# Two decoder layers on one NeuronCore: chunks 0 and 1 become one group that reads its weights once

## The reference, cut to what matters

```python
h = rms(x, g_mix_norm[l])
x = x + mixer_block(h, ...)     # w_in: 1024 x 2816, four mixers of 4 heads, w_out: 1024 x 1024
h = rms(x, g_ffn_norm[l])
x = x + peer(h, w_peer_q[l], sub_keys[l], peer_u[l], peer_v[l])

def peer(h):                    # per chunk of 128 tokens
    q = (xc @ w_q).reshape(C, 8, 2, 128)                  # w_q: 1024 x 2048
    s = einsum('thpd,hpkd->thpk', q, sub_keys)            # 2 x 128 keys a head
    sv, si = top_k(s, 16)                                 # then top 16 of the 16 x 16 sums
    eidx, g = 16 experts of 16384 a head, softmax(top)
    a = einsum('thkd,td->thk', u_tab[eidx], xc)           # gathered rows of 1024
    return einsum('thk,thkd->td', g * gelu(a), v_tab[eidx])
```

## Time and profile before

| | |
|---|---|
| median of 3 runs | 3382.74 us |
| lowest and highest of them | 3364.05 and 3389.28 us |
| the profiled execution, span from first to last instruction | 3383.4 us |
| PE, DVE, POOL, ACT busy | 2560.1, 2327.2, 2291.7, 690.9 us |
| bytes moved | 1205.57 MB |

### The profile page before, as it was taken

The page is one execution under the profiler, slowest core; times in us unless marked ns, Lnnn a source line. Parts: engine busy times, 40 slices in busy tenths (PEclk is TensorE's granted clock), DMA queues, the critical chain, the costliest instruction groups (busy, mean ns, idle before and its releaser), DMA issues.

```text
span 3383.4 us, 27538 instructions
## 1 busy us (share of the span) xinstructions
PE 2560.1 (76%) x7696; PEld 1422.5 (42%) x7696; DVE 2327.2 (69%) x5442; ACT 690.9 (20%) x1655; POOL 2291.7 (68%) x2052
## 2 busy tenths in 40 slices
PE   6568777986777778877787787987787778666667
PEld 5545344743443435533353443643354334222222
DVE  2495678568689875666668886666668888655554
ACT  2112212123311111112211221123322122101011
POOL 0156766566667676676776777677777777777776
PEclk9789888988888888998899998998899899888888
DMA  5489999998899999998999999999999999999998
GB/s 235 174 320 406 358 377 371 343 378 310 308 376 367 347 344 407 401 379 332 352 394 369 379 373 348 390 397 344 348 358 397 363 382 368 368 367 359 366 366 336
DMA packets 316375, 1205.57 MB, mean 356 GB/s; under 512 B 37184, under 2 KB 37440, under 8 KB 301248
## 3 DMA queue, kind: packets, MB, share of 16 engines
q0 software_dynamic: 294912, 1073.87, 83.9%
q1 hardware_dynamic: 21312, 129.94, 9.7%
HBM read 1201.57 MB, written 2.10 MB: 356 GB/s over the span
## 4 chain that ended last, share of the span: by engine, by line
PE 30%; POOL 22%; issue 18%; DVE 17%; DMA 7%; ACT 3%; another core or an unknown queue 2%; SPq 0%; DVEq 0%; ACTq 0%; POOLq 0%
POOL ring L479 22%; PE psY L815 15%; PE psP L694 8%; DMA ring<-in_v,idx 6%; DVE ring L1067 5%; PE psP L689 4%; DVE x L1076 1%; DMA ring<-in_u,idx 1%; DVE sc L860 1%; PE psT L675 1%; ACT diag L656 1%; DVE hot L1031 1%; DVE hot L1032 1%; DVE pick L1033 1%
## 5 line engine op out<-in xcount | busy, mean ns | idle before, releaser
L815 PE MATMUL psY<-ring,diag 128*128 128x512 f32 x3120 | 1689.6, 685 | 678.0 <-DMA ring<-in_v,idx 270.3
L479 POOL DMA_INDIRECT ring<-in_u,idx x1024 | 1148.1, 1121 | 588.1 <-issue 304.3
L1067 DVE CUSTOM_DVE_ANT_0 ring<-ring,htok 128x1024 f32<-128x1024 f32 x1024 | 1232.4, 1223 | 450.5 <-DMA ring<-in_u,idx 396.5
L479 POOL DMA_INDIRECT ring<-in_v,idx x1024 | 1143.3, 1117 | 490.2 <-issue 284.2
L815 PEld LDWEIGHTS psY<-ring,diag 128*128 128x128 f32 x3120 | 636.9, 216 | 1545.9 <-issue 1087.1
L656 ACT ACTIVATE diag<-cst,wgt 128x128 f32<-128x128 f32 x780 | 275.5, 393 | 480.8 <-PE psY L815 184.9
L1076 DVE SCALAR_TENSOR_TENSOR x<-ring,wgt,x 128x1024 f32<-128x1024 f32 x244 | 313.6, 1285 | 39.5 <-DMA ring<-in_v,idx 27.6
L694 PE MATMUL psP<-wr,hT 128*128 128x256 f32 x1392 | 312.7, 383 | 5.1 <-DMA wr<-in_w_out 3.0
L689 PE MATMUL psP<-hT,wr 128*128 128x256 f32 (+1 forms) x1664 | 314.8, 350 | 0.7 <-ACT hT L517 0.7
L689 PEld LDWEIGHTS psP<-hT,wr 128*128 128x128 f32 x1664 | 282.2, 200 | 49.7 <-issue 23.1
L694 PEld LDWEIGHTS psP<-wr,hT 128*128 128x128 f32 x1392 | 267.6, 193 | 65.4 <-issue 22.9
(11 more groups left out here) (125 smaller groups left out, 1652.3 us busy)
## 6 DMA issues: line engine op xcount, KB each, us to landing
wr<-in_w_in SPq DMA_DIRECT2D x44, 1024.0 KB
wr<-in_w_q SPq DMA_DIRECT2D x40, 1024.0 KB
wr<-in_w_out SPq DMA_DIRECT2D x19, 1024.0 KB
ring<-in_u,idx POOLq DMA_INDIRECT x1024
ring<-in_v,idx POOLq DMA_INDIRECT x1024
ring<-in_w_in SPq DMA_DIRECT2D x11, 1024.0 KB, 13.2
x<-in_x SPq DMA_DIRECT2D x4, 512.0 KB, 20.1
sub<-in_subkeys SPq DMA_DIRECT2D x2, 1024.0 KB
```

The lines of the kernel that those rows point to most:

```text
L479: pool.indirect_dma_start(out=ring[:, q % NB], out_offset=None, in_=table, in_offset=bass.IndirectOffsetOnAxis(ap=idx[:, s % NS, n:n + 1], ...
L815: last = nc.tensor.matmul(psY[:, b * 512:(b + 1) * 512], diag[:, m % ND], r[:, b * 512:(b + 1) * 512], start=first, stop=final)
L1067: v.tensor_tensor_reduce(out=r, in0=r, in1=htok[:, s % NS], scale=1.0, scalar=0.0, op0=ALU.mult, op1=ALU.add, accum_out=adot[:, n:n + 1]). ...
```

## The change

The groups (0,) and (1,) become one group (0, 1). Its start slot is -148, where (0,) had -72 and (1,) had 22. Group (2, 3) starts at slot 104 and not 126, with a rate of 0.8 and not 0.7. The groups (4, 5) and (6, 7) are as they were. W_EARLY goes from 12 to 15, so that w_in and w_out of the first group pass through the ring. x of chunk 1 is loaded at the start beside x of chunk 0. (Blank lines at the head of the file go too.)

```diff
@@ -57,14 +38,14 @@
 DV, BV, SU, SV, CB = 4, 5, 6, 7, 8
 
 NB = 12
-W_EARLY = 12
+W_EARLY = 15
 NW = 2
 ND = 4
 NS = 3
 
 
 
-GROUPS = [((0,), -72, 1.0, 1.0), ((1,), 22, 1.0, 0.95), ((2, 3), 126, 0.7, 1.2), ((4, 5), 336, 1.15, 1.3),
+GROUPS = [((0, 1), -148, 1.0, 1.0), ((2, 3), 104, 0.8, 1.2), ((4, 5), 336, 1.15, 1.3),
           ((6, 7), 594, 0.97, 1.5)]
 GROUP_OF = {s: steps for steps, *_ in GROUPS for s in steps}
 
@@ -433,7 +414,8 @@
                 sp.dma_start(gain_f[:], g_ffn[l].partition_broadcast(P)).then_inc(s_late, 16)
                 sp.dma_start(sub[:], subkeys[l]).then_inc(s_late, 16)
 
-            sp.dma_start(x[:, 0], x_in[0:P]).then_inc(s_x[0], 16)
+            for c in range(2):
+                sp.dma_start(x[:, c], x_in[c * P:(c + 1) * P]).then_inc(s_x[c], 16)
             sp.dma_start(cst[:], cst_in).then_inc(s_cst, 16)
             parameters(0)
             for G, (s, i) in enumerate(PIECE_LIST):
@@ -444,7 +426,7 @@
                     late_parameters(l)
                 if G == NB // 2:
                     late_parameters(0)
-                    for c in range(1, NC):
+                    for c in range(2, NC):
                         sp.dma_start(x[:, c], x_in[c * P:(c + 1) * P]).then_inc(s_x[c], 16)
                 place, there, _, used = piece_at(G)
                 if used > 0:
```

## The result

The changed kernel takes 3471.03 us (median of 4 runs, 3463.08 to 3485.64), the kernel before 3383.59 (median of 4, 3364.05 to 3389.28). The ratio is 1.0271, with a 95% interval of 1.0233 to 1.0308. It is slower by some 87 to 92 us; the forecast was 3479, 95 us slower. The profiled execution of the changed kernel took 3463.08 us and has a span of 3461.3, so it is the fastest of its four, and the two spans stand only 77.9 us apart. I come back to that difference.

The account below looks back on a forecast made before the run. A chain of small dependent steps up to the first gather, then a gather stream limited mostly by DMA, was taken as the bound. 3383.4 + 127.4 (later first gather) + 1 - 36 + 3 = 3479 us, range 3440 to 3508.

Parts of the forecast that it names:

- (a) to (d): Before the first gather: later start +9.1, w_in +38.6, chunk 0's attention +4.9, chunk 1's mixers +50.5 us.
- (e) to (g): Before the first gather: w_out +12.4, second norm +8.2, first w_q piece +3.7 us.
- DMA was to stand at 0: Ahead of the stream: DMA at 0 between about 60 and 250 us but for single pieces.
- (d): Before the first gather: chunk 1's mixers, all new on the path, +50.5 us, bounds 40 and 60.
- Slots 0 to 72: Start of the stream: DVE decides, not DMA; 236 us from first gather to slot 72, 235 before, so +1.
- Slots 72 to 123: Stream with no front left in it: 148 us where it took 184, so -36.
- plain pace: Gather stream without front or weights: 1.44 us a gather, 2.88 a slot; 88 us above it before group (2, 3) begins.
- +3 for (2, 3): Group (2, 3) starting 22 slots earlier, its pieces crowding PE: +3 us, bounds 0 and +15.
- Rival 1: DMA sets the whole stream, so bytes count: 23.1 MB fewer give back 58 us, time 3453; chance 0.20.
- price of 1.9 us a piece: Stream between 240 and 340 us: a weight piece cost 1.9 us where DMA was the limit.
- Rival 2: The stream gives nothing back, as DVE choices and earlier (2, 3) pieces crowd it: 3511 us; chance 0.12.
- rival 3: Not slower: chunk 1's mixers run beside chunk 0's and the stream gives 77 us: 3383 us; chance 0.06.

Follow-up runs that it names:

- spread: Changed (merged) kernel with the choices of pairs of group (0, 1) spread over 1.5 times as many slots; ratio to the kernel before 1.0184.
- late23: Changed (merged) kernel with group (2, 3) put back to start slot 126 and rate 0.7; ratio to the kernel before 1.0288.
- thin: Kernel before with the 23 weight loads of chunk 1's group cut to an eighth of their columns, in 128-byte pieces; ratio 1.0014.
- thin1k: Kernel before with the 23 weight loads of chunk 1's group cut to one block of rows, 1 KB a partition; ratio 0.9974.
- delay: Kernel before with 130 DVE copies, about 61 us, put before the first choice of pairs, so the first gather is later; ratio 1.0170.
- mix36: Changed kernel with group (0, 1)'s mixers starting at unit 36, not 50, under the last w_in pieces, start slot -134; ratio to the kernel before 1.0253.
- before_again: Kernel before run once more, unchanged, for a trace from the same chip as other runs; ratio 1.0009.
- combo: Changed kernel with the edits of spread and mix36, and 2 of 16 v rows on DVE for heads 0 to 4, not 4; ratio to the kernel before 1.0156.

## Why the prediction was right

**The bound.** Two stages, with a chain of dependent steps up to the first gather and DMA mostly behind it. The chain of stage one was right in each term to about 2 us. Measured ends: w_in pieces begin at 29.4 (forecast 28.9); the last one ends at 112.8 (112); "stick out" of chunk 0 ends at 142.5 (140.4); that of chunk 1 ends 52.5 behind it (50.5); from the first w_out product to the last addition 30.4 (31.4); from there to w_q 16.1 (16.4); the first w_q piece 9.6 (10.2). The sum was 127.4, and 129.8 and 127.7 were measured in the two pairs. The small errors partly cancel: (a) to (d) came some 4 us above the forecast and (e) to (g) 2 us below. The first w_out piece began at 204.4 and not between 198 and 201. And one sign was wrong: DMA was to stand at 0 from about 60 us on, but had a share of 0.46 from 60 to 80 us and 0.33 from 80 to 100, and stopped only at about 112, as pieces come no sooner than PE frees their places.

**(d), the second chunk's mixers.** It was the largest term and was a sum of pieces, so it is worth a look. Head 1's scores came 9.5 us behind "stick out" (9.6 forecast). The heads followed at 3.81 us (155.83 - 152.02) and 3.89, where I had 3.2: each step works on rows twice as wide, and the two records of the scores took 1.22 us at the lower clock (granted 0.50 from 150 to 165 us, with PE busy for 9.51 of the 15). That makes 1.3 of the 2 us; the rest lies behind the last scores.

**Slots 0 to 72.** Forecast 236, measured 236.1. DVE decides, as was said, but that the number fits to a tenth is luck: the forecast was 10.6 us to the first dot product, 215 of work and 10 of waits, and the trace has 8.3, 209 and 18. Against the kernel before it is -5.6 and not +1, since before needed 241.7; its 235 in the prediction came from 143 records counted in two stretches, one of them twice; by 376 us 71 dot products had begun, and slot 72 began at 382.4. spread shows by experiment that DVE paces this stretch.

**Slots 72 to 123.** Forecast -36, measured -25.5 (178.2 to 152.7). The plain pace is reached only if (2, 3) stays away, as late23 shows (147.0). The +3 for (2, 3) was thus too low up to slot 123; in slots 123 to 144 one pair of traces took 5 us less than before and the other 3 more. Together with slots 0 to 72: forecast -32, measured -31.1 and -31.5. That agreement is luck in part: the errors of the two stretches, 6 to 7 us one way and 10 the other, cancel but for the 3 of (2, 3).

**Behind slot 123.** The prediction had the rest of the stream unchanged and +3 for (2, 3). The crowding of PE by the pieces of (2, 3) did cost 6 to 12 us up to slot 123, but slots 144 to 304 then took 12 to 16 us less, which no term of the prediction has.

**Rival 1 fell**, but not by the result alone: in the two profiled executions of the result the whole stream is 51.9 us shorter, near its 58, and in the pair from one chip 37.7. It fell by thin and thin1k. The bytes were priced at 58 us (61 with the pieces counted right, 96 in the stream before and 73 after, as 19 are read ahead of the first gather in both), and thin1k gives 8.5 and thin nothing for 21.1 MB. The Trainium skill's sentence in "DMA: Bandwidth & Descriptors", section "Issuing engines are not separate DMA queues", agrees with the traces as a statement on the engines: with the weights gone, their share fell from 0.96 and 0.98 in delay to 0.90 and 0.94 in thin1k. But a gain in time needs more, that nothing else waits in that stretch. My own price of 1.9 us a piece, from the rows between 240 and 340 us, was too high as well: 22 pieces would be 42 us. So most of the stream's saving needs the engine work of chunk 1's front to go ahead of the stream. Which engine or wait that work held up between slots 72 and 123 wasn't separated: PE and DVE were each busy for 76% there.

**Rival 2 fell** by the 31 us, and **rival 3** by the first gather: the order of the lists holds, and mix36, which loosens it in one place, has its first gather 7 us sooner.

**The whole.** The stream gave back about 31 us up to slot 123, and 35 up to slot 144 in late23, where (2, 3) stands as it did before (470.4 for 505.1 in thin on the same chip, 505.0 and 505.2 in the traces before); ahead of the stream chunk 1's front costs 128. delay shows that a later start passes through one for one. So each microsecond in front of the first gather was to be paid for by one in the stream, and up to slot 123 the stream had 88 above its plain pace to give at best.

## What to carry to other kernels

Where a long stream is fed by a short chain ahead of it, work placed in the chain cost its full length here (128 us), and the same work in the stream only about 35; price the two places separately, and before a saving of bytes. A DMA share of 0.95 says that transfers are always open and not that they are the bound: cut the bytes in a run of its own. An engine over 90% busy in the same stretch (DVE at 92% in slots 0 to 72 of the changed kernel) is a sign too, but the lack of one is none: in the stretches of the kernel before no engine passed 76%, and the bytes still gave little. And when list-ordered work is spread more thinly in one stretch, look for the stretch that it is pushed into.

## What was not expected of the hardware

The plain pace differs from chip to chip. From 2940 to 3340 us before_again issued 277 gathers, 1.44 us each; on the chip of delay it was 1.30 us (its window from 2860 to 3200). First before_again, then delay, line 479 alone:

```profile
2940.00:3340.00 400.00, 291.37 (x277) 0.83 0.96 363
```

```profile
2860.00:3200.00 340.00, 260.62 (x261) 0.89 1.02 403
```

403 GB/s against 363. The kernel before is 3.3% faster on that chip (3267 against 3378 us), with the start of the stream at the same time. Why the pace differs isn't known. And the faster chip doesn't gain everywhere. Slots 144 to 304 of before_again and of delay, which have the same work there:

```profile
646.70:1180.30 533.60, 407.96 (x1292) 239.84 (x1290) 428.39 (x994) 130.03 (x272) 362.05 (x320) 0.85 0.94 350
698.10:1229.90 531.80, 406.83 (x1292) 239.51 (x1290) 428.31 (x994) 129.64 (x272) 363.15 (x320) 0.86 0.94 349
```

Slots 304 to 1023 took 2185.7 and 2068.9 us, 117 less, and these 160 slots only 2 less, at 350 and 349 GB/s. A chip that gathers 10% faster elsewhere does not do so there, so something other than the speed of its DMA paces that stretch, at a DMA share of 0.94. What it is wasn't looked into. At the plain pace the 160 slots would take 461 us (160 x 2.88), so some 70 us, the weights' own time among them, lie above it there.

The ratio of 1.0156 for combo is from the fast chip and can't be set beside 1.0184 of spread without some caution, as a shorter stream makes the same later start weigh more.
